# A transformer layer on one core: gating before the root, the shift folded into the router's bias, and a reordered tail

## The chip, the core and the metric

The kernel runs on one core of a Trainium2 chip. The metric is the device time of one execution in microseconds (us); before the change it is 1297.55 us, the median of three runs (1297.47 to 1298.02). The engines are TensorE (PE in the rows; its weight loads are PEld), VectorE (DVE), ScalarE (ACT), GpSimd (POOL) and SyncE (SP), which here only issues DMAs. Each runs its own instructions in program order, and waits on semaphores for the others.

## What is computed

One layer over 128 context tokens and 512 latent tokens of width 1024: token mixing (two kinds of attention, an output projection), then a mixture of experts. What the change touches, cut from the reference:

```python
x = x + g1 * rms_norm(merge_branches(oa, ob, ga, gb, p), p['g_post_mix'])
h = rms_norm(x, p['g_pre_ffn']) * (1 + sc) + sh
lg = (t @ p['w_router_group'] + p['b_router_group'])    # t = h, one row per token
le = (t @ p['w_router_expert'] + p['b_router_expert'])
...
return x + gt * rms_norm(hierarchical_moe(h, p), p['g_post_ffn'])
```

`merge_branches` ends in a product with `w_out`. Each token goes to two of 32 experts, each of them three products with a hidden width of 512; `hierarchical_moe` weighs its two results and adds them. An `rms_norm` needs the mean square of a whole row ahead of its root (a power of -0.5).

## The kernel before

The 640 tokens are NT = 5 tiles of 128 rows, one token on each of 128 partitions. Everything is written out by hand, engine by engine; there is no scheduler, and the order of each engine's work is that of its block of code. The stages that count here:

- **Output projection.** TensorE makes the merged rows in two halves of 512 columns (n = 0 and 1), each by two units of weights and five tiles. Every product is three matmuls (high and low parts of fp32). ScalarE copies a finished tile's half into `yr` and squares it (`merged_rows`, `y_cp`).
- **Between projection and router**, the *row stage* below. For each tile VectorE adds the halves' mean squares; GpSimd takes the root ("merged root", `yrs`); VectorE multiplies by root and gate and adds the old x (`new_x`, two instructions); ScalarE squares the new x (`x1_squares`); VectorE adds EPS; GpSimd takes the second root ("x root", `x1rs`); VectorE scales (`scaled_h`, signals `h2_part`) and adds the shift (`shifted_h`, signals `h2_done`). GpSimd's code has the merged root and the x root of a tile one behind the other, then those of the next tile.
- **Router.** TensorE transposes h (`transpose_h2`, eight matmuls for a tile), ScalarE copies the columns out (`h2_columns`, half of the last tile by VectorE), TensorE multiplies them by the router's weights (`router`), ScalarE copies the 36 logits of each token (`logit_rows`) and TensorE turns them back (`logits`). When all five are there (`rl_done`), VectorE picks the experts and makes the tables of rows to gather.
- **Loads.** SyncE's queue loads 1 MB units of expert weights into six slots. Slots 0 to 2 have their own place. Slots 3 to 5 (`raw_extra`) lie where `yr` and the gate and shift rows are, so their first loads wait until h is stored to memory (`h2_out`) and transposed. GpSimd's gathers read that stored h, and also wait for `h2_out`.
- **Experts.** For each of the 32 experts six weight units are split into high and low parts (ScalarE, then VectorE), and multiplied.
- **Tail.** Five loads of 1 MB bring each token's two results; VectorE weighs the first (`c_part`), adds the weighed second (`c_sum`), ScalarE squares (`c_sq`), GpSimd takes one root over all five tiles (`c_rs`), and VectorE multiplies by root and gate and adds x, in two instructions for each tile; SyncE stores the tile.

## Time and profile before

| | |
|---|---|
| median of three runs | 1297.55 us |
| the profiled execution, its device time | 1295.41 us |
| its span in the trace | 1293.7 us |
| busy: TensorE, VectorE, ScalarE, GpSimd | 1145.2, 848.7, 688.4, 311.1 us |
| mean granted TensorE clock | 0.95 of full speed |

The span runs from the first to the last instruction or transfer of the trace; the profiled execution took 1.7 us more than its span. All positions below are microseconds from the span's start. The row stage and the router lie at about 596 to 638, the experts at about 662 to 1250, the tail at 1255 to the end. A busy share says little here: what counts is, in each stage, which engine the others wait for.

### The profile page before, as it was taken

How to read it: one execution, taken by the hardware profiler on the slowest of the kernel's cores; microseconds unless marked ns; L12 is line 12 of the kernel's file. 1: busy time of each engine (PE TensorE's matmuls, PEld its weight loads, DVE VectorE, ACT ScalarE, POOL GpSimd, SP SyncE). 2: the span in 40 equal slices, each digit the busy share in tenths (PEclk: the TensorE clock that was granted, in tenths of full speed). 3: DMA queues.
4: the chain of work that ended last, by engine and by line, in shares of the span. 5: the costliest groups of instructions: out<-in, count | busy, mean ns of one | idle time of the engine just before them, and what ended most of it. 6: DMA issues, size and time to landing. Idle time of an engine off the chain costs nothing. (4 is left out here: it accounts for less than half of the span.)

```text
span 1293.7 us, 16787 instructions
## 1 busy us (share of the span) xinstructions
PE 1145.2 (89%) x5927; PEld 919.8 (71%) x5927; DVE 848.7 (66%) x901; ACT 688.4 (53%) x781; POOL 311.1 (24%) x306
## 2 busy tenths in 40 slices
PE   4889999999788989998559999999999999999950
PEld 2567788778566777886448788888888888888830
DVE  3543133113787654515739899889898999888936
ACT  3222223223565541234337777877888778877721
POOL 4022021010113002000112443334433344334200
PEclk9889999999898999999769999999999999999985
DMA  9634434555001116421549999999999999999924
GB/s 314 229 98 147 140 119 144 179 171 179 18 1 54 63 33 222 130 73 49 191 171 353 374 376 377 375 364 357 357 364 358 356 356 364 370 352 362 362 67 197
DMA packets 146028, 296.38 MB, mean 229 GB/s; under 512 B 12097, under 2 KB 13250, under 8 KB 145330
## 3 DMA queue, kind: packets, MB, share of 16 engines
q1 hardware_dynamic: 130656, 265.83, 57.7%
q0 software_dynamic: 15152, 29.73, 6.9%
q8 instruction: 36, 0.59, 0.2%
q14 instruction: 22, 0.18, 0.0%
q10 hardware_dynamic: 162, 0.05, 0.0%
HBM read 290.68 MB, written 27.95 MB: 246 GB/s over the span
## 5 line engine op out<-in xcount | busy, mean ns | idle before, releaser
L1192 PE MATMUL psum<-w_hi,act_hi 128*128 128x512 f32 (+1 forms) x1288 | 517.2, 402 | 22.9 <-DVE w_lo L1887 6.3
L1194 PE MATMUL psum<-w_hi,act_lo 128*128 128x512 f32 (+1 forms) x1288 | 502.7, 390 | 0.0
L1193 PE MATMUL psum<-w_lo,act_hi 128*128 128x512 f32 (+1 forms) x1288 | 502.0, 390 | 0.0
L1192 PEld LDWEIGHTS psum<-w_hi,act_hi 128*128 128x128 f32 x1288 | 244.5, 190 | 96.1 <-issue 18.1
L1194 PEld LDWEIGHTS psum<-w_hi,act_lo 128*128 128x128 f32 x1288 | 244.7, 190 | 51.9
L1193 PEld LDWEIGHTS psum<-w_lo,act_hi 128*128 128x128 f32 x1288 | 245.4, 191 | 45.4
L1887 DVE TENSOR_TENSOR w_lo<-raw_extra,w_hi 128x2048 fp32r<-128x2048 f32 x96 | 217.2, 2289 | 45.9 <-ACT w_hi L1082 45.9
L1887 DVE TENSOR_TENSOR w_lo<-raw_mix,w_hi 128x2048 fp32r<-128x2048 f32 x96 | 219.3, 2288 | 12.3 <-ACT w_hi L1082 12.2
L1082 ACT ACTIVATE w_hi<-raw_mix 128x2048 fp32r<-128x2048 f32 x96 | 183.9, 1916 | 27.0 <-PE psum L1194 27.0
L1082 ACT ACTIVATE w_hi<-raw_extra 128x2048 fp32r<-128x2048 f32 x96 | 180.5, 1913 | 7.0 <-PE psum L1194 7.0
L1599 DVE TENSOR_TENSOR w_lo<-raw_mix,w_hi 128x2048 fp32r<-128x2048 f32 (+1 forms) x24 | 52.9, 2202 | 164.5 <-ACT w_hi L882 164.5
L830 POOL DMA_INDIRECT y_scratch<-ysb,scatter_column x32 | 32.6, 1017 | 358.2 <-DVE ysb L2024 347.5
L882 ACT ACTIVATE w_hi<-raw_mix 128x2048 fp32r<-128x2048 f32 (+1 forms) x24 | 44.2, 1842 | 64.1 <-PE psum L1194 37.9
L818 POOL DMA_INDIRECT xg<-h_scratch,gather_column x32 | 69.7, 2177 | 26.1 <-POOL gather_column L815 24.9
L825 POOL COPY scatter_column<-scatter_rows 128x1 uint32 (+1 forms) x32 | 58.1, 1816 | 0.0
L815 POOL COPY gather_column<-gather_rows 128x1 uint32 (+1 forms) x32 | 51.7, 1615 | 21.4 <-DVE gather_rows L1987 16.6
L1013 ACT ACTIVATE rows<-psum,soft 128x640 f32<-128x640 f32 (+3 forms) x80 | 50.7, 641 | 8.1 <-DVE soft L1774 6.1
L1143 ACT ACTIVATE act_hi<-psum 128x512 fp32r<-128x512 f32 x32 | 19.2, 599 | 55.7 <-PE psum L1553 55.7
L1381 PE MATMUL psum<-ident,rows 128*128 128x128 f32 x204 | 38.4, 297 | 10.6 <-DVE pt L1821 4.7
L1772 DVE TENSOR_REDUCE soft<-psum 128x2 f32<-128x1280 f32 (+3 forms) x40 | 44.3, 1109 | 3.7 <-PE psum L1362 1.8
L2004 DVE TENSOR_TENSOR act_lo<-psum,act_hi 128x1024 fp32r<-128x1024 f32 x32 | 39.0, 1219 | 10.9 <-ACT act_hi L1125 10.9
L1125 ACT ACTIVATE act_hi<-psum 128x1024 fp32r<-128x1024 f32 x32 | 32.8, 1025 | 21.2 <-PE psum L1523 21.2
(273 smaller groups left out, 1143.1 us busy)
## 6 DMA issues: line engine op xcount, KB each, us to landing
raw_mix<-in_w_e SPq DMA_DIRECT2D x96, 1024.0 KB, 8.2
raw_extra<-in_w_e SPq DMA_DIRECT2D x96, 1024.0 KB, 8.2
raw_mix<-in_w_in SPq DMA_DIRECT2D x16, 1024.0 KB, 5.8
raw_mix<-in_w_ada SPq DMA_DIRECT2D x16, 1024.0 KB, 7.0
ada_first<-in_w_ada SPq DMA_DIRECT2D x8, 1024.0 KB, 20.3
gates_scratch<-rows POOLq DMA_DIRECT2D x20, 256.0 KB, 3.2
yrow<-gates_scratch POOLq DMA_DIRECT2D x20, 256.0 KB, 4.6
raw_mix<-in_w_out SPq DMA_DIRECT2D x4, 1024.0 KB, 5.1
```

Source lines behind the costliest of these rows:

```text
L815: po.tensor_copy(idx_g[:, par:par + 1], tab_g[:, bass.ds(n, 1)]).then_inc(gi_done, 1)
L818: po.indirect_dma_start(out=xg[:, par * D:(par + 1) * D], out_offset=None, in_=h2_d, in_offset=bass.IndirectOffsetOnAxis(idx_g[:, par:par ...
L825: po.tensor_copy(idx_s[:, par:par + 1], tab_s[:, bass.ds(n, 1)]).then_inc(si_done, 1)
L882: ac.activation(whi(s % HL)[:, :, 0:w], raw(n % RAW_MIX)[:, :, 0:w], ACT.Copy).then_inc(hi_done, 1)
L1013: ac.activation(e[:, m * w:(m + 1) * w], s_view(i)[:, m, :], ACT.Exp, bias=soft[:, 16 * b + m:16 * b + m + 1], scale=SCALE, accum_out=tota ...
L1082: ac.activation(whi(hl), raw(slot), ACT.Copy).then_inc(hi_done, 1)
L1192: pe.matmul(out, a_hi(ka_), w_hi[:, kw, :], start=s, stop=False)
L1193: pe.matmul(out, a_hi(ka_), w_lo[:, kw, :], start=False, stop=False)
L1194: ins = pe.matmul(out, a_lo(ka_), w_hi[:, kw, :], start=False, stop=e)
L1599: ve.tensor_tensor(wlo(s % HL)[:, :, 0:w], raw(n % RAW_MIX)[:, :, 0:w], whi(s % HL)[:, :, 0:w].bitcast(F32), ALU.subtract).then_inc(lo_don ...
L1772: link(ve.reduce_max(so[:, 8:10], s_view(i), AX.X))
L1887: ve.tensor_tensor(wlo(hl), raw(slot), whi(hl).bitcast(F32), ALU.subtract).then_inc(lo_done, 1)
```

## The change

It has three parts.

1. **Row stage.** VectorE now multiplies each half of the merged rows by the gate as soon as it is copied (`gated`, 512 columns), ahead of the root, which makes `new_x` one instruction. The shift is taken off the router's path: TensorE transposes the scaled rows (it waits for `h2_part`), and the shift's part of the logits, shift times the router's weights, is made by eight small matmuls after the first unit of the projection (`rt_mm` then counts one more), copied by ScalarE (`shl`), and added as the bias of `logit_rows`. VectorE still adds the shift to the rows that are stored, but behind each tile's transposes, three of the five behind the copy of the last columns.
2. **Order.** GpSimd takes the merged root of tile i ahead of the x root of tile i - 1. ScalarE splits its second expert unit (`early(0, [1])`) ahead of the second half's rows, and squares and copies in another order. TensorE has the transposes of tile 4 ahead of router 3. VectorE's low part of that second expert unit (`moe_lo(NS + 2, 1, 0)`) moves behind the making of the tables.
3. **Tail.** ScalarE weighs the first result (`first_part`), VectorE adds the second and at once multiplies by the gate into another place (`c_gate`), and behind the root there is one instruction for each tile (`final_rows`).

The diff, without declarations and changed counts:

```diff
-            for i in range(NT):
+            def merged_root(i):
                 po.wait_ge(ysum, i + 1)
                 po.tensor_tensor(stat[:, 8 + i:9 + i], stat[:, i:i + 1], half[:, 0:1], ALU.pow).then_inc(yrs, 1)
+
+            def x1_root(i):
                 po.wait_ge(xsum, i + 1)
                 po.tensor_tensor(stat[:, 40 + i:41 + i], stat[:, 32 + i:33 + i], half[:, 0:1], ALU.pow).then_inc(x1rs, 1)
+
+            merged_root(0)
+            for i in range(1, NT):
+                merged_root(i)
+                x1_root(i - 1)
+            x1_root(NT - 1)
...
@@ -1092,28 +1102,31 @@
                 merged_rows(0, i)
             split_hi(25)
             early(0, [0])
+            ac.wait_ge(rt_mm, 1)
+            link(ac.activation(shl[0:NR, :], bank(7)[0:NR, 0:2], ACT.Copy))
+            early(0, [1])
             for i in range(NT):
                 merged_rows(1, i)
-                if i:
+                if 0 < i < NT - 1:
                     x1_squares(i - 1)
-                if i == 1:
-                    early(0, [1])
 
                     ac.wait_ge(rl_done, i - 1)
-                ac.activation(rlT[:, i % 2 * P:(i % 2 + 1) * P], bank(2 + i % 2)[0:NR, 0:P], ACT.Copy).then_inc(rt_cp, 1)
+                ac.activation(rlT[:, i % 2 * P:(i % 2 + 1) * P], bank(2 + i % 2)[0:NR, 0:P], ACT.Identity, bias=shl[0:NR, min(i, 1):min(i, 1) + 1]).then_inc(rt_cp, 1)
 
             h2_columns(0)
+            x1_squares(NT - 2)
             h2_columns(1)
+            logit_rows(0)
+            h2_columns(2)
             x1_squares(NT - 1)
-            h2_columns(2)
-            logit_rows(0)
+            logit_rows(1)
+            logit_rows(2)
             h2_columns(3)
-            for i in range(1, NT - 1):
-                logit_rows(i)
             h2_columns(NT - 1)
+            logit_rows(3)
             logit_rows(NT - 1)
...
-            for i in range(NT):
+            def first_part(i):
+                ac.wait_ge(x_in[i], 32)
+                y0 = raw_pair(i)[:, 0:D]
+                ac.activation(y0, y0, ACT.Copy, scale=wk[:, i:i + 1]).then_inc(c_part, 1)
+
+            def pair_squares(i):
                 ac.wait_ge(c_sum, i + 1)
                 if i:
                     ac.wait_ge(c_sq, i)
                 ac.activation(pt[:, 1024:2048], raw_pair(i)[:, 0:D], ACT.Square, accum_out=stat[:, i:i + 1]).then_inc(c_sq, 1)
+
+            first_part(0)
+            for i in range(1, NT):
+                first_part(i)
+                pair_squares(i - 1)
+            pair_squares(NT - 1)
...
+                    if n == 0 and u == 0:
+                        shift = modc[:, :].rearrange("p (j s) -> p j s", s=2)
+                        for k in range(KD):
+                            ins = pe.matmul(bank(7)[0:NR, 0:2], wr_v[:, k, :], shift[:, 24 + k, :], start=(k == 0), stop=(k == KD - 1))
+                        ins.then_inc(rt_mm, 1)
 
             def transpose_h2(i):
-                pe.wait_ge(h2_done, i + 1)
+                pe.wait_ge(h2_part, i + 1)
...
             transpose_h2(2)
             router(1)
             logits(0)
-            transpose_h2(3)
             router(2)
             logits(1)
+            transpose_h2(3)
+            logits(2)
+            transpose_h2(4)
             router(3)
-            logits(2)
+            router(4)
             logits(3)
-            transpose_h2(4)
-            router(4)
             logits(4)
...
             moe_lo(NS + 1, 0, 2)
-            ve.wait_ge(y_cp, 5)
+            ve.wait_ge(b_in, 16 * 6)
+
+            def gated(n, i):
+                ve.wait_ge(y_cp, 5 * n + i + 1)
+                half_row = yr[:, i, n * 512:n * 512 + 512]
+                ve.tensor_tensor(half_row, half_row, br_v[:, min(i, 1), n * 512:n * 512 + 512], ALU.mult).then_inc(mix_done, 1)
+
+            for i in range(NT):
+                gated(0, i)
             link(ve.tensor_scalar(stat[:, 48:53], stat[:, 48:53], EPS, None, ALU.add))
+
+            def merged_mean_square(i):
+                ve.wait_ge(y_cp, 5 + i + 1)
+                ve.tensor_tensor(stat[:, i:i + 1], stat[:, 48 + i:49 + i], stat[:, 53 + i:54 + i], ALU.add).then_inc(ysum, 1)
+
+            def mean_square(i):
+                ve.wait_ge(x1sq, i + 1)
+                ve.tensor_scalar(stat[:, 32 + i:33 + i], stat[:, 32 + i:33 + i], EPS, None, ALU.add).then_inc(xsum, 1)
+
+            def new_x(i):
+                ve.wait_ge(yrs, i + 1)
+                ve.wait_ge(x2_in[i], 16)
+                ve.wait_ge(mix_done, 4 * NT + NT + i + 1)
+                ve.scalar_tensor_tensor(xrow[:, i, :], yr[:, i, :], stat[:, 8 + i:9 + i], xrow[:, i, :], ALU.mult, ALU.add).then_inc(x1_done, 1)
 
             def scaled_h(i):
                 ve.wait_ge(x1rs, i + 1)
                 ve.scalar_tensor_tensor(yr[:, i, :], xrow[:, i, :], stat[:, 40 + i:41 + i], br_v[:, 2 + min(i, 1), :], ALU.mult, ALU.mult).then_inc(h2_part, 1)
 
             def shifted_h(i):
-                ve.wait_ge(h2_part, i + 1)
+                ve.wait_ge(h2t_done, 2 * i + 2)
...
-            ve.wait_ge(b_in, 16 * 6)
-            def mean_square(i):
-                ve.wait_ge(x1sq, i + 1)
-                ve.tensor_scalar(stat[:, 32 + i:33 + i], stat[:, 32 + i:33 + i], EPS, None, ALU.add).then_inc(xsum, 1)
-
-            def new_x(i):
-                ve.wait_ge(yrs, i + 1)
-                link(ve.scalar_tensor_tensor(yr[:, i, :], yr[:, i, :], stat[:, 8 + i:9 + i], br_v[:, min(i, 1), :], ALU.mult, ALU.mult))
-                ve.wait_ge(x2_in[i], 16)
-                ve.tensor_tensor(xrow[:, i, :], xrow[:, i, :], yr[:, i, :], ALU.add).then_inc(x1_done, 1)
-
+            merged_mean_square(0)
             for i in range(NT):
-                ve.wait_ge(y_cp, 5 + i + 1)
-                ve.tensor_tensor(stat[:, i:i + 1], stat[:, 48 + i:49 + i], stat[:, 53 + i:54 + i], ALU.add).then_inc(ysum, 1)
-                if i >= 2:
-                    shifted_h(i - 2)
+                gated(1, i)
                 if i:
                     mean_square(i - 1)
                 new_x(i)
+                if i + 1 < NT:
+                    merged_mean_square(i + 1)
                 if i:
                     scaled_h(i - 1)
             mean_square(NT - 1)
-            shifted_h(NT - 2)
+            shifted_h(0)
             scaled_h(NT - 1)
-            shifted_h(NT - 1)
+            shifted_h(1)
             ve.wait_ge(h2t_done, 2 * NT)
-            ve.wait_ge(rt_mm, NT - 2)
+            ve.wait_ge(rt_mm, 1 + NT - 2)
             ve.tensor_copy(h2T_v[(NT - 1) % 2][:, 512:1024], bank(h2_bank(NT - 1, 1))).then_inc(h2t_v, 1)
-            moe_lo(NS + 2, 1, 0)
+            for i in range(2, NT):
+                shifted_h(i)
...
+            moe_lo(NS + 2, 1, 0)
...
-            for i in range(NT):
+            def pair_sum(i):
                 ve.wait_ge(x_in[i], 32)
+                ve.wait_ge(c_part, i + 1)
                 y2 = raw_pair(i)
-                ve.tensor_scalar(y2[:, 0:D], y2[:, 0:D], wk[:, i:i + 1], None, ALU.mult).then_inc(c_part, 1)
-                ve.wait_ge(c_part, i + 1)
                 ve.scalar_tensor_tensor(y2[:, 0:D], y2[:, D:2 * D], wk[:, NT + i:NT + i + 1], y2[:, 0:D], ALU.mult, ALU.add).then_inc(c_sum, 1)
-            ve.wait_ge(c_rs, 1)
+                ve.wait_ge(c_sum, i + 1)
+                ve.tensor_tensor(y2[:, D:2 * D], y2[:, 0:D], g2_v[:, min(i, 1), :], ALU.mult).then_inc(c_gate, 1)
+
+            def final_rows(i):
+                ve.wait_ge(c_rs, 1)
+                ve.wait_ge(c_gate, i + 1)
+                ve.scalar_tensor_tensor(xrow[:, i, :], raw_pair(i)[:, D:2 * D], stat[:, 8 + i:9 + i], xrow[:, i, :], ALU.mult, ALU.add).then_inc(c_out, 1)
+
             ve.wait_ge(g2_in, 32)
             for i in range(NT):
-                y2 = raw_pair(i)
-                ve.scalar_tensor_tensor(y2[:, 0:D], y2[:, 0:D], stat[:, 8 + i:9 + i], g2_v[:, min(i, 1), :], ALU.mult, ALU.mult).then_inc(c_part, 1)
-                ve.wait_ge(c_part, NT + i + 1)
-                ve.tensor_tensor(xrow[:, i, :], xrow[:, i, :], y2[:, 0:D], ALU.add).then_inc(c_out, 1)
+                pair_sum(i)
+            for i in range(NT):
+                final_rows(i)
```

VectorE's instructions of two tiles in the middle of the row stage, before; `yrow` is `yr`, `rows` is x, `brow` holds the gate, scale and shift rows, `stat` the mean squares and roots:

```order
L1904 TENSOR_SCALAR stat<-stat 128x1
L1908 SCALAR_TENSOR_TENSOR yrow<-yrow,stat,brow 128x1024
L1910 TENSOR_TENSOR rows<-rows,yrow 128x1024
L1895 SCALAR_TENSOR_TENSOR yrow<-rows,stat,brow 128x1024
L1914 TENSOR_TENSOR stat<-stat 128x1
L1899 TENSOR_TENSOR yrow<-yrow,brow 128x1024
L1904 TENSOR_SCALAR stat<-stat 128x1
L1908 SCALAR_TENSOR_TENSOR yrow<-yrow,stat,brow 128x1024
L1910 TENSOR_TENSOR rows<-rows,yrow 128x1024
L1895 SCALAR_TENSOR_TENSOR yrow<-rows,stat,brow 128x1024
L1914 TENSOR_TENSOR stat<-stat 128x1
L1899 TENSOR_TENSOR yrow<-yrow,brow 128x1024
```

And with the change, over the same two tiles:

```order
L1946 SCALAR_TENSOR_TENSOR yrow<-rows,stat,brow 128x1024
L1924 TENSOR_TENSOR yrow<-yrow,brow 128x512
L1936 TENSOR_SCALAR stat<-stat 128x1
L1942 SCALAR_TENSOR_TENSOR rows<-yrow,stat,rows 128x1024
L1932 TENSOR_TENSOR stat<-stat 128x1
L1946 SCALAR_TENSOR_TENSOR yrow<-rows,stat,brow 128x1024
L1924 TENSOR_TENSOR yrow<-yrow,brow 128x512
L1936 TENSOR_SCALAR stat<-stat 128x1
L1942 SCALAR_TENSOR_TENSOR rows<-yrow,stat,rows 128x1024
L1932 TENSOR_TENSOR stat<-stat 128x1
```

The shift's addition and the second instruction of the new x are gone from the loop; a half-width product with the gate has come in.

TensorE's instructions from the last projection product to the last logits, before (`ident` marks transposes, `wr` the router's products):

```order
L1466 MATMUL psum<-ident,yrow 128x128 x16
L1475 MATMUL psum<-h2T,wr 36x128 x8
L1466 MATMUL psum<-ident,yrow 128x128 x8
L1475 MATMUL psum<-pt,wr 36x128 x8
L1480 MATMUL psum<-ident,orow 128x36
L1466 MATMUL psum<-ident,yrow 128x128 x8
L1475 MATMUL psum<-h2T,wr 36x128 x8
L1480 MATMUL psum<-ident,orow 128x36
L1475 MATMUL psum<-pt,wr 36x128 x8
L1480 MATMUL psum<-ident,orow 128x36 x2
L1466 MATMUL psum<-ident,yrow 128x128 x8
L1475 MATMUL psum<-h2T,wr 36x128 x8
L1480 MATMUL psum<-ident,orow 128x36
```

And with the change:

```order
L1495 MATMUL psum<-ident,yrow 128x128 x16
L1504 MATMUL psum<-h2T,wr 36x128 x8
L1495 MATMUL psum<-ident,yrow 128x128 x8
L1504 MATMUL psum<-pt,wr 36x128 x8
L1509 MATMUL psum<-ident,orow 128x36
L1504 MATMUL psum<-h2T,wr 36x128 x8
L1509 MATMUL psum<-ident,orow 128x36
L1495 MATMUL psum<-ident,yrow 128x128 x8
L1509 MATMUL psum<-ident,orow 128x36
L1495 MATMUL psum<-ident,yrow 128x128 x8
L1504 MATMUL psum<-pt,wr 36x128 x8
L1504 MATMUL psum<-h2T,wr 36x128 x8
L1509 MATMUL psum<-ident,orow 128x36 x2
```

The transposes of tile 3 now stand behind router 2, and those of tile 4 ahead of routers 3 and 4, which follow each other.

VectorE's end of the program, before, from the last two tiles' sums on:

```order
L2052 TENSOR_SCALAR raw_extra<-raw_extra,pair_weights 128x1024
L2054 SCALAR_TENSOR_TENSOR raw_extra<-raw_extra,pair_weights 128x1024
L2059 SCALAR_TENSOR_TENSOR raw_mix<-raw_mix,stat,last_gate_rows 128x1024
L2061 TENSOR_TENSOR rows<-rows,raw_mix 128x1024
L2059 SCALAR_TENSOR_TENSOR raw_mix<-raw_mix,stat,last_gate_rows 128x1024
L2061 TENSOR_TENSOR rows<-rows,raw_mix 128x1024
```

And with the change:

```order
L2094 SCALAR_TENSOR_TENSOR raw_extra<-raw_extra,pair_weights 128x1024
L2096 TENSOR_TENSOR raw_extra<-raw_extra,last_gate_rows 128x1024
L2101 SCALAR_TENSOR_TENSOR rows<-raw_mix,stat,rows 128x1024 x3
L2101 SCALAR_TENSOR_TENSOR rows<-raw_extra,stat,rows 128x1024 x2
```

Two instructions for each tile behind the root have become one, and the gate's product stands ahead of it.

## Rows read from the trace of the kernel before

**Rows 1.** The stretches view: busy us of each engine, clock, DMA share, GB/s.

```profile
595.00:605.00 10.00, 10.00 (x46) 8.29 (x45) 4.16 (x6) 6.34 (x11) 1.63 (x3) 1.00 0.01 2
615.00:625.00 10.00, 6.03 (x30) 4.96 (x31) 7.60 (x10) 3.10 (x7) 2.10 (x4) 0.54 0.26 105
```

**Rows 2.** The timeline of VectorE: start, us, line, operation, idle before and releaser.

```profile
609.96 1.28 DVE L1908 SCALAR_TENSOR_TENSOR yrow<-yrow,stat,brow 128x1024 f32<-128x1024 f32 x1 [1.17 <-POOL stat L802]
611.28 1.22 DVE L1910 TENSOR_TENSOR rows<-rows,yrow 128x1024 f32<-128x1024 f32 x1
612.42 1.28 DVE L1895 SCALAR_TENSOR_TENSOR yrow<-rows,stat,brow 128x1024 f32<-128x1024 f32 x1
...
616.18 1.29 DVE L1908 SCALAR_TENSOR_TENSOR yrow<-yrow,stat,brow 128x1024 f32<-128x1024 f32 x1 [1.17 <-POOL stat L802]
...
626.25 1.22 DVE L1899 TENSOR_TENSOR yrow<-yrow,brow 128x1024 f32<-128x1024 f32 x1
...
637.54 0.34 DVE L1934 TENSOR_TENSOR router_logits<-psum,br 128x180 f32<-128x180 f32 x1 [0.46 <-PE psum L1480]
```

**Rows 3.** The timeline of ScalarE: merged rows, tiles 0 and 1; squares.

```profile
596.33 0.60 ACT L1061 ACTIVATE yrow<-psum 128x512 f32<-128x512 f32 x1 [11.39 <-PE psum L1194]
...
599.05 0.60 ACT L1061 ACTIVATE yrow<-psum 128x512 f32<-128x512 f32 x1 [1.40 <-PE psum L1194]
...
612.53 1.06 ACT L1068 ACTIVATE pt<-rows 128x1024 f32<-128x1024 f32 x1 [3.88 <-DVE rows L1910]
```

**Rows 4.** The timeline of GpSimd: the x roots of tiles 3 and 4.

```profile
621.33 0.54 POOL L804 TENSOR_TENSOR stat<-stat,half 128x1 f32<-128x1 f32 x1 [5.18 <-DVE stat L1904]
...
626.41 1.46 POOL L804 TENSOR_TENSOR stat<-stat,half 128x1 f32<-128x1 f32 x1 [4.03 <-DVE stat L1904]
```

**Rows 5.** The timeline of TensorE: router products, transposes, first expert product.

```profile
620.94 3.51 PE L1475 MATMUL psum<-h2T,wr 128*36 128x128 f32 x16 [3.96 <-ACT h2T L1075]
...
624.38 1.09 PE L1466 MATMUL psum<-ident,yrow 128*128 128x128 f32 x8
625.40 1.94 PE L1475 MATMUL psum<-pt,wr 128*36 128x128 f32 x16
...
662.50 0.79 PE L1192 MATMUL psum<-w_hi,act_hi 128*128 128x512 f32 x1 [2.44 <-DVE act_lo L2004]
```

**Rows 6.** The timeline of TensorE: four products two columns wide, early on.

```profile
195.06 0.95 PE L1228 MATMUL psum<-fold_parts,modulation_row_parts 128*128 128x2 f32 x8
```

**Rows 7.** Groups by line and form: GpSimd copies one column (busy, mean ns).

```profile
L815 POOL COPY gather_column<-gather_rows 128x1 uint32 x30 | 51.3, 1710 | 4.8 <-PE psum L1523 4.7
```

**Rows 8.** The waits between 680 and 1240: us in total, times, longest.

```profile
ACT w_hi L1082 <- PE psum L1194: 27.0, 61, 0.8
```

**Rows 9.** The timeline of SyncE's queue: the first loads behind the stored h.

```profile
634.25 1.49 SPq L596 DMA_DIRECT2D raw_extra<-in_w_e  x3
```

**Rows 10.** The gathered tile `xg`, all its gathers.

```profile
DMA to landing us min/median/max: 4.4/8.1/8.7
```

**Rows 11.** The timeline of VectorE in the tail.

```profile
1273.39 0.75 DVE L2052 TENSOR_SCALAR raw_extra<-raw_extra,pair_weights 128x1024 f32<-128x1024 f32 x1 [0.38 <-DMA raw_extra<-y_scratch]
1274.18 1.28 DVE L2054 SCALAR_TENSOR_TENSOR raw_extra<-raw_extra,pair_weights 128x1024 f32<-128x1024 f32 x1
1278.27 1.28 DVE L2059 SCALAR_TENSOR_TENSOR raw_mix<-raw_mix,stat,last_gate_rows 128x1024 f32<-128x1024 f32 x1 [2.80 <-POOL stat L695]
...
1289.40 1.22 DVE L2061 TENSOR_TENSOR rows<-rows,raw_extra 128x1024 f32<-128x1024 f32 x1
```

**Rows 12.** The timeline of GpSimd in the tail: the root over five tiles.

```profile
1277.03 1.21 POOL L695 TENSOR_TENSOR stat<-stat,half 128x5 f32<-128x5 f32 x1
```

**Rows 13.** One line's view: ScalarE scales rows by a column, durations min, median, max.

```profile
L919 ACT ACTIVATE rows<-rows,stat x3: 1133/1134/1135, 14.8 to 16.9; 128x1024 f32<-128x1024 f32 x3
```

**Rows 14.** One line's view: the output stores of the tail.

```profile
DMA to landing us min/median/max: 2.6/2.6/2.6
```

**Rows 15.** The stretches view, two microseconds of the output stores.

```profile
1284.00:1286.00 2.00, 0.00 (x0) 0.00 (x0) 1.97 (x3) 0.00 (x0) 0.00 (x0) 0.50 0.65 262
```

20 lines of the change are left out of this document (11 added, 9 removed).

## The prediction

> **What bounds the kernel now.** I read the strip of 40 slices first, then each stage by stretches and timelines. Three parts of the program matter.
>
> The experts, 662 to 1250, hold the most time, and the change edits nothing in them. There ScalarE, when it waits to split a weight unit, waits for TensorE to give a buffer back, never for a load [rows 8]: TensorE sets the pace, and the stage's length stays as it is if it begins earlier and the weights are there. So a gain ahead of it reaches the end in full.
>
> The row stage ahead of it is VectorE's. Between 615 and 625 VectorE is busy for 7.60 of 10 us, ScalarE for 3.10, and TensorE works on at half clock, 0.54 on the mean, after it had stood mostly idle; between 595 and 605, under the projection, TensorE was busy throughout at 1.00 [rows 1]. From one tile's new x (609.96) to the next (616.18) it takes 6.22 us, at whose end VectorE still sits idle for 1.17 us until GpSimd's root [rows 2]. GpSimd could have made it long before: its code has the x root of the tile ahead in front, and so waits 5.18 us for a sum [rows 4]. TensorE delivers a tile each 2.72 us (599.05 less 596.33) [rows 3], so the stage could run more than twice as fast. The stage ends when VectorE takes the last logits, at 637.54 [rows 2]; from there to the first expert product, at 662.50 [rows 5], lie the tables and the first gather.
>
> The tail is one chain: last load, sum, squares, root, then ten VectorE instructions one behind the other, from 1278.27 to 1290.62 (1289.40 and 1.22) [rows 11].
>
> **The row stage, worked out.** Of a tile's VectorE work two instructions of 1.22 leave the loop, the add of old x and the shift [rows 2]; a gate product of half that width comes in, some 0.6. What is left, with starts closer by 0.08 than durations, is gate 0.6, two small ones of 0.1, new x 1.2 and scaling 1.2, thus 3.2. To that comes a wait for the x root. The one root that ran beside a long VectorE instruction took 1.46 instead of 0.54 [rows 4]; that instruction began at 626.25 and ended at 627.47 [rows 2], so the root ended 0.40 behind it. Now nearly every root runs so: 3.2 and 0.4 make 3.6 a tile.
>
> I walked all four engines' new orders with these durations (the same walk over the old orders ends at 637.7, where the trace has 637.54). The small products delay all by their own length. Four with 128-column weights take 0.95 [rows 6]; eight with 36-column weights lie between 0.6 (their weights being narrower) and 1.94, which is eight router products with 128 columns of data [rows 5]. I take 1.2, as for the data they are nearest to the first row. New x of tile 0 then begins at 600.1, and that of tile 4 at 600.1 + 2.7 + 3 x 3.6 = 613.7. Behind it: new x 1.3, squares 1.06 and their read-out, together 1.2 [rows 3], sum and hand-overs 0.7, root 1.5, scaling 1.3, to 619.7; then transposes 1.1 and routers 3 and 4 at 1.9 each [rows 5], to 624.6; copy, last logits and hand-overs 0.7: **625.3**. The order that puts two routers behind the last transposes costs one more router there (1.9), but the copy by VectorE hides in the first of them. Against 637.54 that is 12.3 less, and 11.7 to 13.0 for the bounds of the small products alone.
>
> Costed at nothing: the gate products of the first half (3 us under the projection's second half, where VectorE is idle more than half of the time [rows 1]); the second unit's split by ScalarE, moved to before the second half's rows, where it waits for weights' buffers freed in time (else it would delay the first rows by up to 1.9); the five shifts, of which two lie in waits of VectorE and three (3.5 us) beside routers 3 and 4 (3.8 us). Without that cover they would come in full ahead of the tables. ScalarE's bias in the logits may cost 0.1.
>
> What the shift's move makes late: stored h. Loads for slots 3 to 5 stood at 634.25, 3.3 ahead of the last logits [rows 9]; now the last store is issued at 624.8, the logits' time, and lands 3.3 later (2.6 for a store of this size [rows 14] and a queue of stores). So weights start 6.6 us later against the router, and 6 only ahead of before. SyncE's queue has the later units behind them, and slot 1's reload now waits for the low part that moved behind the tables. All six have landed about when TensorE starts, and none but slot 3's is needed within the first 10 us. But the first gather now meets a full stream. All gathers land in 4.4 to 8.7, median 8.1 [rows 10], and the first one already met one unit of weights; I add 0.3, at most 0.6. GpSimd's clearing of `xg` (it waits for `h2_done`) now falls onto the tables' small VectorE instructions: 0 to 1.8, the latter if they wait for all of it; I take 0.3, as each of them is short.
>
> The clock: behind the projection TensorE gets work of 1.1 to 1.9 us with gaps under a microsecond, and I expect 1.00 to hold up to the last logits. At the experts' start it comes back at half clock either way; by which matmul it rises may move by 1 us. Left at nothing. **Row stage: 12.3 - 0.6 = 11.7, bounds 9.5 to 14.**
>
> **The tail.** ScalarE's weighing has the form of a row that takes 1.13 [rows 13], against 0.75 on VectorE [rows 11], and the last sum begins behind it and one gate product: at 1274.6 instead of 1274.18, so the last squares come 0.4 later. The last gate product (1.2) lies beside those squares, ahead of the root of 1.21 [rows 12]. Final rows begin at 1278.7 instead of 1278.27; five instructions at 1.2 end at 1284.8 instead of 1290.62: 5.9 less. Now stores come each 1.2. At 262 GB/s the transfers took 0.65 of the DMA engines [rows 15], which makes 403 GB/s in full and 1.3 for the 0.52 MB of one tile. From the first store at 1280.0: 2.6 and 4 x 1.3 give 1287.8, where VectorE's last rows alone would give 1287.4, and before it was 1293.3. **Tail: 5.5, bounds 4.5 to 5.9.**
>
> **Sum.** 11.7 + 5.5 = 17.2. Against the profiled execution (span 1293.7, time 1295.41) that gives a span of 1276.5. The median of the runs, 1297.55, is 2.1 above that execution; the saving is the same: **1280.4**.
>
> **A rule against the change.** GpSimd's roots stretch when VectorE is busy, 0.54 to 1.46, and during the experts a copy of one column takes 1.71 on the mean [rows 4, 7]; my sum has 1.5 for most roots. The Trainium skill (GPSIMD Engine Reference, Key points) says that GpSimd shares its SBUF interfaces with VectorE and contends with its instructions in a two-port mode or with two SBUF inputs. New x, gate and scaling all have two SBUF inputs, so by that rule every root may be held; the trace agrees in direction, and no row shows how far it goes when VectorE has no gap. With no root held the walk ends 0.5 earlier; with each held to 2.0, a whole 1.28 and its own time, it ends at 629.2, and the time is 1284.3. How it would be beyond that is the second rival.
>
> **Rivals.**
> - *The weights set the start.* If the experts had no slack in loads, the gain of the row stage would be the loads' 6 us, not 11.7, and the time 1297.55 - 6 - 5.5 = 1286. For it: the loads start late. Against: rows 8, and units not needed at once. 0.12.
> - *GpSimd starved: slower.* Ten roots stand in one line, so the stage ends at about 609 + 10 x the mean root, once that passes 2 us. With 3.4 the whole gain, tail included, is gone; with 4 it is 1304. For it: the stretched rows. Against: the mean there, under instructions of 2.3, is 1.71 [rows 7]. 0.03.
> - *The clock falls during the router.* If TensorE works at half clock from 611 on, router products take 3.51 [rows 5]; walked through, logits end at 635.6, and with the tail the time is 1290. For it: it fell in just this place before. Against: the gaps that did it are gone. 0.08.
> - *It does not do what it says:* with GpSimd or ScalarE in the way the stage keeps its 6.2 and the tail's gain is eaten by stores. Within 0.2%: 0.02.
>
> **How the numbers follow.** The forecast has 0.75. Its own range is 17.2 with the bounds: low 1297.55 - 14 - 5.9 = 1277.6, and 1 less for the clock's rise; high 1297.55 - 9.5 - 4.5 = 1283.6. The 8-in-10 range takes in the weights' rival: 1276.6 to 1287. A difference of 0.2%, 2.6 us, is about what can be told from none. Faster 0.95, same 0.02, slower 0.03.
>
> **What would show it.** New x each 3.6 us and last logits near 625 (with the first row's time the same, within 0.5); roots of 1 to 1.6; TensorE's clock at 1.00 between 608 and 625; first expert product near 651; experts' stage as long as before; final rows 1.2 apart and an end 9.5 us behind the tail's root instead of 15.5. I am wrong if a root takes over 2 us, if the clock falls ahead of 625, or if ScalarE waits for loads.

## The result, and the profile after

| | before | after |
|---|---|---|
| first comparison, median of four runs each | 1297.78 us (1297.47 to 1299.06) | 1276.63 us (1274.88 to 1277.12) |
| ratio after / before, 95% interval | | 0.9834 [0.9819, 0.985] |
| profiled execution, its span | 1295.41, 1293.7 us | 1276.24, 1274.5 us |

Faster by 21.2 us in this comparison, where 17.2 was forecast; the spans of the two traces differ by 19.2 us. Two more comparisons, below, gave 20.8 and 17.8.

**Stretches of the changed kernel** (us busy and, in brackets, instructions of PE, PEld, DVE, ACT, POOL; then granted clock, DMA share, GB/s). They answer to [rows 1]:

```profile
605.00:615.00 10.00, 9.00 (x68) 7.62 (x67) 9.44 (x16) 8.69 (x19) 4.83 (x6) 1.00 0.00 0
615.00:625.00 10.00, 8.20 (x68) 7.16 (x66) 8.67 (x14) 4.67 (x8) 2.92 (x2) 1.00 0.58 233
625.00:635.00 10.00, 1.61 (x30) 1.19 (x30) 8.73 (x27) 0.16 (x1) 0.27 (x2) 0.57 0.78 275
```

TensorE and VectorE are both busy up to the last logits and the clock holds at full (2.4 GHz). It falls to half in the next stretch, when TensorE has nothing but small work for the tables.

**VectorE and GpSimd in the row stage**, timelines of the changed kernel (start, us, engine, line), which answer to [rows 2] and [rows 4]:

```profile
604.37 0.68 DVE L1924 TENSOR_TENSOR yrow<-yrow,brow 128x512 f32<-128x512 f32 x1
604.97 0.14 DVE L1936 TENSOR_SCALAR stat<-stat 128x1 f32<-128x1 f32 x1
605.18 1.28 DVE L1942 SCALAR_TENSOR_TENSOR rows<-yrow,stat,rows 128x1024 f32<-128x1024 f32 x1
606.45 1.28 DVE L1946 SCALAR_TENSOR_TENSOR yrow<-rows,stat,brow 128x1024 f32<-128x1024 f32 x1
608.46 1.28 DVE L1942 SCALAR_TENSOR_TENSOR rows<-yrow,stat,rows 128x1024 f32<-128x1024 f32 x1
...
619.81 3.49 DVE L1950 TENSOR_TENSOR yrow<-yrow,brow 128x1024 f32<-128x1024 f32 x3
623.52 0.35 DVE L1974 TENSOR_TENSOR router_logits<-psum,br 128x180 f32<-128x180 f32 x1 [0.22 <-PE psum L1509]
```

```profile
605.19 0.54 POOL L808 TENSOR_TENSOR stat<-stat,half 128x1 f32<-128x1 f32 x1 [1.47 <-DVE stat L1936]
606.61 1.52 POOL L804 TENSOR_TENSOR stat<-stat,half 128x1 f32<-128x1 f32 x1 [0.88 <-DVE stat L1932]
608.47 0.54 POOL L808 TENSOR_TENSOR stat<-stat,half 128x1 f32<-128x1 f32 x1 [0.34 <-DVE stat L1936]
```

The middle tiles take 3.28 us each (605.18 to 608.46), not 3.6: there is no wait ahead of the scaling at 606.45. The merged root (L804) starts while a scaling runs and ends at 608.13, 0.40 behind that scaling's end (606.45 and 1.28), as in [rows 4]. But the x root (L808) starts within 0.01 us of a new x and takes its bare 0.54. One round earlier the forecast wait is there, and that round took 3.75 us (new x at 601.43 and 605.18):

```profile
601.30 0.15 DVE L1936 TENSOR_SCALAR stat<-stat 128x1 f32<-128x1 f32 x1 [0.32 <-ACT pt L1078]
601.43 1.28 DVE L1942 SCALAR_TENSOR_TENSOR rows<-yrow,stat,rows 128x1024 f32<-128x1024 f32 x1
601.53 1.59 POOL L808 TENSOR_TENSOR stat<-stat,half 128x1 f32<-128x1 f32 x1
603.15 1.29 DVE L1946 SCALAR_TENSOR_TENSOR yrow<-rows,stat,brow 128x1024 f32<-128x1024 f32 x1
```

Here the x root starts 0.10 us into the new x and ends at 603.12; only then can the scaling start. The last three shifts lie beside the last router products. The logits come at 623.52, against 637.54 in [rows 2].

**TensorE**, timeline of the changed kernel; the rows from 606 on answer to [rows 5], the first are the small products:

```profile
565.25 0.72 PE L1483 MATMUL psum<-modc,wr 128*36 128x2 f32 x16
...
606.84 2.04 PE L1495 MATMUL psum<-ident,yrow 128*128 128x128 f32 x16
609.88 1.94 PE L1504 MATMUL psum<-h2T,wr 128*36 128x128 f32 x16 [1.00 <-ACT h2T L1085]
611.75 1.09 PE L1495 MATMUL psum<-ident,yrow 128*128 128x128 f32 x8
...
648.82 0.79 PE L1216 MATMUL psum<-w_hi,act_hi 128*128 128x512 f32 x1 [2.44 <-DVE act_lo L2045]
```

The small products take 0.72 us where 1.2 was put in. One wait of 1.00 us ahead of router 0 does not cost the clock. The first expert product comes 25.30 us behind the logits, 24.96 before.

**The experts' waits**, 665 to 1220, and SyncE's timeline ahead of them, which answer to [rows 8] and [rows 9]:

```profile
ACT w_hi L1092 <- PE psum L1218: 26.8, 61, 0.8
```

```profile
615.90 7.74 SPq L626 DMA_DIRECT2D h_scratch<-yrow  x5
626.68 1.49 SPq L598 DMA_DIRECT2D raw_extra<-in_w_e  x3
```

ScalarE still waits for TensorE alone, in 61 places as before, though slots 3 to 5 are loaded 3.2 us behind the logits instead of 3.3 ahead of them: the weights do not set the start.

**The tail**, timeline of the changed kernel, which answers to [rows 11, 12]:

```profile
1262.20 1.23 DVE L2096 TENSOR_TENSOR raw_extra<-raw_extra,last_gate_rows 128x1024 f32<-128x1024 f32 x1
...
1263.72 1.21 POOL L697 TENSOR_TENSOR stat<-stat,half 128x5 f32<-128x5 f32 x1
1264.97 3.68 DVE L2101 SCALAR_TENSOR_TENSOR rows<-raw_mix,stat,rows 128x1024 f32<-128x1024 f32 x3 [1.54 <-POOL stat L697]
...
1267.47 3.92 SPq L653 DMA_DIRECT2D out_y_sample<-rows  x4
1268.56 2.47 DVE L2101 SCALAR_TENSOR_TENSOR rows<-raw_extra,stat,rows 128x1024 f32<-128x1024 f32 x2
```

Final rows come each 1.2 us. From the issue of the first load to the end it is 32.50 us (1242.00 to 1274.5); it was 37.98 (1255.72 to 1293.7): 5.48 less. Part of that stretch is the loads' own time, which differs from trace to trace. Counted from the first instruction that the last load released it is 20.31 us before and 14.88 now; over all traces below with the old tail 20.25 to 20.33, over the eight with this one 14.81 to 14.92.

### The profile page after: what moved, and what is told of

It reads as the page before. It is cut to its first block and busy times, and to the rows that moved or that the text cites. A ratio compares the mean times of both kernels' runs of the same rounds, so it can differ in the third digit from the quotient of the medians.

```text
span 1274.5 us, 16835 instructions
## 1 busy us (share of the span) xinstructions
PE 1141.1 (90%) x5943; PEld 917.4 (72%) x5943; DVE 844.3 (66%) x901; ACT 694.7 (55%) x787; POOL 316.1 (25%) x306
## 5 line engine op out<-in xcount | busy, mean ns | idle before, releaser
L825 POOL COPY gather_column<-gather_rows 128x1 uint32 (+1 forms) x32 | 52.7, 1648 | 13.8 <-DVE gather_rows L2027 9.7
L1156 ACT ACTIVATE act_hi<-psum 128x512 fp32r<-128x512 f32 x32 | 19.2, 599 | 55.5 <-PE psum L1582 55.5
```

What stands on the lines that cost most here:

```text
L825: po.tensor_copy(idx_g[:, par:par + 1], tab_g[:, bass.ds(n, 1)]).then_inc(gi_done, 1)
```

## The experiments

Executions of one kernel spread by several us, while the row stage, where its code is the same, repeats within 0.02 us from trace to trace. So each trace was cut at the same five places of its timelines: GpSimd's first merged root (A), VectorE taking the last logits (B), first expert product (C), issue of the tail's first load (D), end of the span (E). The other stretches repeat less well: over all kernels here B to C lies between 24.80 and 26.36, C to D between 592.66 and 594.47, and D to E with the changed tail between 31.18 and 33.67. All in us; the ratio is to before on the same chip.

| kernel | A at | A to B | B to C | C to D | D to E | median | ratio, 95% |
|---|---|---|---|---|---|---|---|
| before | 598.02 | 39.52 | 24.96 | 593.22 | 37.98 | | |
| after | 597.82 | 25.70 | 25.30 | 593.18 | 32.50 | 1276.63 | 0.9834 [0.9819, 0.985] |
| e1 before again | 597.71 | 39.53 | 25.36 | 592.66 | 37.34 | 1295.05 | 1.0004 [0.9993, 1.0016] |
| e2 tail only | 598.75 | 39.54 | 24.99 | 593.01 | 32.51 | 1291.19 | 0.9967 [0.9954, 0.998] |
| e3 rows only | 599.71 | 25.69 | 25.53 | 593.18 | 37.59 | 1282.89 | 0.9894 [0.9881, 0.9908] |
| e4 old root order | 598.61 | 28.99 | 26.34 | 593.03 | 32.43 | 1280.63 | 0.9881 [0.9866, 0.9895] |
| e5 after again | 597.63 | 25.70 | 26.36 | 592.98 | 31.63 | 1276.21 | 0.9839 [0.9811, 0.9866] |
| e6 gate undone | 598.63 | 29.87 | 25.18 | 593.30 | 32.52 | 1281.06 | 0.9875 [0.9845, 0.9905] |
| e7 shift on path | 599.71 | 30.44 | 24.80 | 594.47 | 31.18 | 1282.91 | 0.9885 [0.9845, 0.9925] |
| e8 roots by parts | 598.55 | 25.70 | 25.24 | 593.81 | 34.50 | 1278.95 | 0.9857 [0.9827, 0.9886] |
| e9 old PE and ACT order | 596.73 | 31.48 | 25.36 | 593.83 | 32.40 | 1285.95 | 0.9923 [0.9906, 0.994] |
| e10 held store | 599.65 | 25.71 | 25.60 | 593.57 | 33.77 | 1278.93 | 0.9854 [0.9836, 0.9873] |
| e11 two parts | 604.19 | 25.71 | 25.58 | 593.50 | 32.12 | 1278.41 | 0.9854 [0.9838, 0.9871] |
| e12 store after loads | 596.84 | 25.71 | 25.67 | 593.45 | 31.03 | 1275.22 | 0.9856 [0.9833, 0.9879] |
| e13 after again | 601.04 | 25.71 | 25.15 | 593.73 | 33.67 | 1276.91 | 0.9859 [0.9839, 0.9879] |

**e1: the kernel before, unchanged.**

> The kernel before, unchanged, to see how one program's executions differ. The forecast's 1297.55 - 17.2 took over the 2.1 us between the profiled execution and the median of before; with the change the two differ by 0.4 only. Theory A (chance between executions, of any kernel): single times spread over 1295 to 1298, and another profile lands anywhere in it. Rival B (TensorE's clock in the row stage of before, which falls and rises in it): times differ by where the clock rises, and the profile shows half clock for another length than 13.7 us in 600 to 640. Ratio to before 1.000 in both.

1295.05 us in the median of 12 executions, 1293.89 to 1300.92. That spread is wider than expected; its A to B is that of the first trace (39.53 and 39.52) and the clock between 600 and 640 falls and rises as there, which speaks for theory A. The kernel's two sets on this chip have medians 2.2 and 2.7 us below that of the first comparison.

**e2: the tail alone.** All of part 3 of the change, the row stage as before.

> The kernel before with the new tail alone (ScalarE weighs, gate ahead of the root, one instruction behind it). Mine: from the first load's issue to the end 32.5 us instead of 38.0, so 5.5 less, 1292.2, last rows at 1.2 a tile and stores as the bound. Rival: the tail is worth the 2 us more that were measured than traced, 7.5 less, 1290.2.

4.4 us faster than before by the medians (5.5 expected), and D to E 32.51, as in the whole change (37.98 before). The rival's 7.5 us lies outside the interval of the ratio (2.6 to 6.0 us).

**e3: the row stage alone.** Parts 1 and 2, the tail as before.

> The changed kernel with the old tail. Mine: the row stage and what follows it give all the rest, last logits near 623.5 and about 1282.1 (1276.6 + 5.5). If the missing 2 us belong to the tail instead: 1284.

12.7 us faster by the medians; A to B 25.69, that of the whole change (25.70). With e2's 4.4 that makes 17.1 of medians that each are uncertain by 1.5 or so; by stages, 13.8 and 5.5.

**e4: the roots in the old order.**

```diff
-            merged_root(0)
-            for i in range(1, NT):
-                merged_root(i)
-                x1_root(i - 1)
-            x1_root(NT - 1)
+            for i in range(NT):
+                merged_root(i)
+                x1_root(i)
```

> The changed kernel with GpSimd's roots in the old order (x root of a tile ahead of the next tile's merged root). Mine: each new x then waits for two roots in a row; by the walk a tile takes 4.6 instead of 3.3, last logits come 3.8 later (627.5) and the time is 1280.4. Rival: GpSimd is not in the way, since VectorE's own work of 3.2 a tile sets the pace, and TensorE's router work afterwards takes up what is late: within 0.5 of 1276.6.

A to B 28.99, 3.29 more (3.8 expected), at 4.39 a tile: 3.3 us of the stage hang on the order of the roots, and the rival falls. GpSimd's timeline shows it, the x root in front and the merged root right behind it:

```profile
606.73 0.55 POOL L808 TENSOR_TENSOR stat<-stat,half 128x1 f32<-128x1 f32 x1 [3.33 <-DVE stat L1934]
607.25 0.54 POOL L804 TENSOR_TENSOR stat<-stat,half 128x1 f32<-128x1 f32 x1
```

**e5 and e13: the changed kernel, unchanged.**

> The changed kernel once more, unchanged, on the same chip as the three that follow. Theory A (the traces of the two profiled executions hold the whole effect, 19.2 us, and the other 2 us of the first comparison were the executions of before, which spread from 1293.9 to 1300.9 and stood high in that session): the ratio to before is about 0.985, the gain 19 to 19.5 us, and from the first merged root to the last logits the trace shows 25.7 us again, as against 39.5 in before. Theory B (the change gains the 21 us of the first comparison, and the profiled execution of before was a lucky one): ratio 0.9835, a gain over 20.5.

> The changed kernel beside the version above on one chip, in five rounds. Theory A: a gain of 19 to 19.5 us over before as the median of many executions, ratio 0.985, the trace's root to logits 25.7 again. Theory B: ratio 0.9835, gain over 20.5. The share of the 21.2 us that neither trace explains (2.0) is then the spread of the executions ahead of the row stage (the first merged root came between 596.7 and 604.2 us in the eleven kernels run so far, in code that none of them changes but for the small products) or something of the change.

20.8 and 17.8 us faster than before in their own sets, 21.2 in the first. The interval of e5 holds the ratios of both theories, that of e13 (0.9839 to 0.9879) leaves out theory B's 0.9835. The medians of before went from 1294.66 to 1297.78 between sets (four of them on different chips), those of the changed kernel only from 1276.21 to 1276.91; chips and chance are not told apart. All executions together, 58 of before (one stray of 4543.68 us left out) and 13 of the changed kernel, have medians of 1295.69 and 1276.44: 19.25 us, near what the traces say (19.2), though 29 of the 58 ran on a chip where the changed kernel did not. About 19 us is the best figure. Part of the spread is seen ahead of the row stage. Two traces, e1 (A at 597.71) and e11 (A at 604.19), by stretches:

```profile
300.00:400.00 100.00, 83.17 (x569) 67.52 (x567) 71.78 (x175) 54.08 (x124) 15.96 (x32) 0.95 0.10 35
400.00:500.00 100.00, 86.65 (x667) 72.23 (x668) 60.33 (x152) 44.11 (x131) 12.24 (x23) 0.91 0.26 90
```

```profile
300.00:400.00 100.00, 86.94 (x575) 70.73 (x571) 71.37 (x172) 53.85 (x123) 14.74 (x30) 0.90 0.10 38
400.00:500.00 100.00, 84.89 (x644) 70.95 (x643) 60.66 (x153) 45.55 (x135) 12.44 (x23) 0.86 0.21 73
```

The clock granted between 300 and 500, where TensorE works with gaps, is 0.95 and 0.91 in the one, 0.90 and 0.86 in the other, in code that no kernel here changes. It is not all: e3 and e10 have 0.95 and 0.91 there too, and their row stages began 2.0 us behind that of e1.

**e6: the gate behind the root again.**

```diff
-            for i in range(NT):
-                gated(0, i)
...
-                ve.wait_ge(x2_in[i], 16)
-                ve.wait_ge(mix_done, 4 * NT + NT + i + 1)
-                ve.scalar_tensor_tensor(xrow[:, i, :], yr[:, i, :], stat[:, 8 + i:9 + i], xrow[:, i, :], ALU.mult, ALU.add).then_inc(x1_done, 1)
+                link(ve.scalar_tensor_tensor(yr[:, i, :], yr[:, i, :], stat[:, 8 + i:9 + i], br_v[:, min(i, 1), :], ALU.mult, ALU.mult))
+                ve.wait_ge(x2_in[i], 16)
+                ve.tensor_tensor(xrow[:, i, :], xrow[:, i, :], yr[:, i, :], ALU.add).then_inc(x1_done, 1)
...
-                gated(1, i)
```

> The changed kernel with the gate put back into VectorE's row loop as two full rows of work (root times gate, then the sum with x), and no gating by halves; all else as changed. Theory A (VectorE's list of work sets the period of a tile): one 1.2 us instruction more on a row and one 0.7 us instruction less, and the sum can't start before both: period 4.3 instead of 3.28, first merged root to last logits 29.4 us instead of 25.7, so 3.7 us slower than changed. Theory C (GpSimd's two roots set the period, VectorE fits in beside): period stays near 3.3 and the stage within 0.5 us.

A to B 29.87, 4.17 more (3.7 expected), at 4.24 a tile. VectorE's list sets the period; theory C falls. The clock fell here too, behind waits of 2.47 and 1.00 us:

```profile
611.16 1.09 PE L1495 MATMUL psum<-ident,yrow 128*128 128x128 f32 x8 [2.47 <-DVE yrow L1939]
613.25 3.28 PE L1504 MATMUL psum<-h2T,wr 128*36 128x128 f32 x16 [1.00 <-ACT h2T L1085]
616.46 1.37 PE L1495 MATMUL psum<-ident,yrow 128*128 128x128 f32 x8
```

TensorE had no wait from there to the last transposes, at 623.05, for which the scaled rows had been ready since 622.58. So it lost 1.6 us here (3.28 and 1.37 instead of 1.94 and 1.09) and most of that was made good by what it would have waited for anyway; some 0.4, about what the forecast lacks, is left (an estimate from these rows).

**e7: the shift ahead of the transposes again**, without small products and bias.

```diff
                 gated(1, i)
+                if i >= 2:
+                    shifted_h(i - 2)
...
-                pe.wait_ge(h2_part, i + 1)
+                pe.wait_ge(h2_done, i + 1)
```

> The changed kernel with the shift added to every row before its transposes again, and without the sixteen small products and the bias on the logits' copies; all else as changed. Theory A: VectorE's list gets 1.15 us longer a tile, period 4.4 instead of 3.28, first merged root to last logits 28.8 us instead of 25.7, so 3.1 us slower than changed; the small products taken away give back at most the 0.7 us that they last. Theory C (TensorE, which is nearly without gaps from the first router product, sets the end whatever VectorE does): within 1 us of changed.

A to B 30.44, 4.74 more instead of 3.1, at 4.70 to 4.74 a tile instead of 4.4. Its timelines of GpSimd and VectorE:

```profile
612.93 1.54 POOL L808 TENSOR_TENSOR stat<-stat,half 128x1 f32<-128x1 f32 x1 [2.69 <-DVE stat L1929]
```

```profile
612.70 0.15 DVE L1929 TENSOR_SCALAR stat<-stat 128x1 f32<-128x1 f32 x1
612.76 1.28 DVE L1935 SCALAR_TENSOR_TENSOR rows<-yrow,stat,rows 128x1024 f32<-128x1024 f32 x1
613.96 0.17 DVE L1925 TENSOR_TENSOR stat<-stat 128x1 f32<-128x1 f32 x1
614.50 1.28 DVE L1939 SCALAR_TENSOR_TENSOR yrow<-rows,stat,brow 128x1024 f32<-128x1024 f32 x1 [0.38 <-POOL stat L808]
```

Here new x starts 0.06 behind the small instruction (612.76), the x root 0.17 behind new x, and is held to 614.47, so that VectorE waits 0.38: the very wait that the prediction had put into the changed kernel. There, in the middle tiles, new x starts 0.21 behind the small instruction, as it waits for its own gate product just ahead; the root gets in at the same moment and is not held. In the changed kernel's first round the gate product had ended 0.3 us before the small instruction, new x started 0.13 behind that, and the root was held. TensorE waited 3.08 us, came back at half clock, and did tile 1's transposes in 1.97 us instead of 1.1:

```profile
612.84 1.97 PE L1488 MATMUL psum<-ident,yrow 128*128 128x128 f32 x8 [3.08 <-DVE yrow L1943]
614.74 2.42 PE L1497 MATMUL psum<-h2T,wr 128*36 128x128 f32 x16
...
624.80 1.09 PE L1488 MATMUL psum<-ident,yrow 128*128 128x128 f32 x8 [0.82 <-DVE yrow L1943]
```

That did not lengthen the stage: ahead of the last transposes TensorE waits 0.82 us for VectorE again. VectorE's longer round, its waits for the root included, and the last tile's shift are what the stage was longer by.

**e9: TensorE's and ScalarE's lists in the old order**, VectorE, GpSimd and the rest as changed.

```diff
             logits(0)
+            transpose_h2(3)
             router(2)
             logits(1)
-            transpose_h2(3)
-            logits(2)
-            transpose_h2(4)
             router(3)
-            router(4)
+            logits(2)
             logits(3)
+            transpose_h2(4)
+            router(4)
             logits(4)
```

> The changed kernel with TensorE's and ScalarE's lists in the row stage in the order of before (transposes of tile 3 ahead of router 2, those of tile 4 behind router 3 and logits 3; ScalarE's squares of new rows 3 inside the row loop, of rows 4 between the column copies); VectorE, GpSimd, gates by halves and small products as changed. Theory A (with VectorE's list short, TensorE's order sets when the last logits can come): first merged root to last logits 31.0 us as against 25.7, the new x of tile 2 some 1.3 us later because its tile's roots wait for ScalarE; 5.3 us slower than changed. Theory F (the orders only follow VectorE's, and each engine would wait as long in either): within 0.7 us of changed.

The diff shows TensorE's part; ScalarE's squares of tiles 3 and 4 go back to where they were. A to B 31.48, the largest share of all (5.78, expected 5.3). New x keeps its pace of 3.29, also that of tile 2, which had been expected 1.3 later; what is late is behind it. TensorE's timeline, and the stretches around it:

```profile
610.87 2.80 PE L1502 MATMUL psum<-h2T,wr 128*36 128x128 f32 x16 [3.08 <-ACT h2T L1085]
613.60 1.85 PE L1493 MATMUL psum<-ident,yrow 128*128 128x128 f32 x8
```

```profile
605.00:610.00 5.00, 2.79 (x20) 2.19 (x19) 4.93 (x9) 3.62 (x8) 3.24 (x3) 1.00 0.00 0
610.00:615.00 5.00, 4.13 (x23) 3.58 (x24) 4.48 (x7) 3.19 (x7) 2.32 (x3) 0.68 0.00 0
```

A wait of 3.08 us, then half clock for 3 to 4 us: the rival "the clock falls during the router" is real, and the row names what keeps it off: ScalarE's column copy of tile 0, which the change has ahead of the squares of tile 3, and before had behind them. Counted from A, router 0 starts 2.1 us later than in the changed kernel and router 1 3.7 later, after two pieces at half clock; the other 2.1 of the 5.8 come after that. So the larger part goes back to one place in ScalarE's list. What TensorE's order is worth by itself no run shows, as e9 moves both lists.

**e8: roots in three parts in the tail**, ScalarE's squares of pair 0 ahead of the weighing of pair 1, VectorE's final rows of pair 0 ahead of the sum of pair 1.

```diff
-            po.wait_ge(c_sq, NT)
-            rsqrt(stat[:, 8:8 + NT], stat[:, 0:NT], NT, 1.0 / D).then_inc(c_rs, 1)
+            for a, b in ((0, 1), (1, NT - 1), (NT - 1, NT)):
+                po.wait_ge(c_sq, b)
+                rsqrt(stat[:, 8 + a:8 + b], stat[:, a:b], b - a, 1.0 / D).then_inc(c_rs, 1)
```

> The changed kernel with another order in the tail: GpSimd takes the root of pair 0 as soon as its squares are summed, those of pairs 1 to 3 together, that of pair 4 last; ScalarE squares pair 0 before it weighs pair 1; VectorE writes the final rows of pair 0 before it sums pair 1, when it waits for that pair's load anyway. Theory A (VectorE sets the tail's end: 2.5 us for each pair from the second one's landing, then 1.2 for each final row not yet written): one final row moves into the wait for the load and one into the wait for the last root; the last row ends 26.5 us after the first load's issue instead of 29.0, the kernel 2.3 to 3.2 us faster than changed. Theory D (a root is held while VectorE works, so that the one for pairs 1 to 3 ends only 0.4 us after the last gate product, and the last root 0.5 later still): gain 1.5 to 2 us only. Theory E (the stores set the end): no gain.

The last row ended 27.80 us behind D (29.03 in the changed kernel's first trace), but the end came later, not earlier: 34.50; the median is 2.7 us above that of e5, which ran on the same chip. SyncE's waits in its tail (L88 stands for the program's closing code):

```profile
SPq L88 <- PEq L88: 3.5, 1, 3.5
SPq L88 <- DMA out_y_sample<-rows: 2.5, 1, 2.5
```

Behind the last landing the program waited 3.5 us more, 0.2 in every kernel with one root. A to B is the changed kernel's.

**e10: the same with the first store held back.**

```diff
-                sp.wait_ge(c_out, i + 1)
+                sp.wait_ge(c_out, max(i + 1, 2))
```

> The roots by parts once more, with the store of the first final rows held until the second are written, so that no store is among the pairs' loads. Theory A (that store's 512 KB at the loads' pace delayed pairs 3 and 4 by about 1.2 us and so all of VectorE's list behind): last row ends about 27.1 us after the first load's issue, as against 27.8 with the early store and 28.2 to 29.0 as changed. Of the 3.3 us between the last landing and the end, which the roots by parts had more than the changed kernel: gone with the early store (theory G), or still there, as it belongs to the longer program (theory H). By G the kernel is 1 to 2 us faster than changed, by H 1 to 2 slower.

Last row 27.11 behind D, as expected (that store had delayed the loads: ScalarE waited 1.1 us for the fourth pair in e8, 0.3 here), but the closing wait stayed, at 2.2 us: G falls.

**e11: roots in two parts, (0) and (1 to 4).**

> As the held store, with roots in two parts only: pair 0 as soon as it is squared, pairs 1 to 4 together at the end. Theory A: the last root starts as VectorE ends its last gate product and is not held (1.2 us), four final rows come behind it instead of five: last row ends 27.8 us after the first load's issue, 1.2 less than changed, and the kernel is 1.2 us faster, if the end after the last landing is as in the changed kernel (H says it is 3.3 longer whenever the tail's order is another; G says it isn't).

Closing wait 0.2, last row 27.48 behind D, yet D to E 32.12: with five stores issued from 1272.90 on, the end came 8.2 us behind the first of them (1281.1), as in the changed kernel (1266.28 to 1274.5). H falls in its simple form too; the stores set the end.

**e12: two parts, and the first store when the last load has landed.**

```diff
+                if i == 0:
+                    sp.wait_ge(x_in[NT - 1], 32)
                 sp.wait_ge(c_out, i + 1)
```

> Roots in two parts, and the store of the first final rows issued as soon as the last pair's load has landed, where the transfers stood still for 10 us in the changed kernel. Theory I (once VectorE writes a final row each 1.2 us, five stores of 512 KB follow one another without a gap and set the end: it came 8.2 us after the first of the five issues in the changed kernel and in the two-part one alike): four stores are left behind the last root, so the end comes at 30.9 us from the first load's issue, as against 32.5 as changed. Theory K (the program can't end earlier than 8.5 us after GpSimd's last instruction: both three-part kernels ended 8.6 to 8.7 us after it, and SyncE waited there for something of TensorE's queue for 3.5 and 2.2 us after the last landing): GpSimd's last root ends 22.6 us from the load's issue, so the end comes at 31.2 to 31.3 and SyncE's last wait is 0.4 to 0.7 instead of 0.2. Kernel 1.2 to 1.6 us faster than changed. If last rows set the end instead: no more than two parts gave.

Timelines of GpSimd and SyncE, and SyncE's waits:

```profile
1263.05 1.03 POOL L699 TENSOR_TENSOR stat<-stat,half 128x4 f32<-128x4 f32 x1
```

```profile
1258.94 0.34 SPq L655 DMA_DIRECT2D out_y_prompt<-rows  x1
...
1265.42 2.72 SPq L655 DMA_DIRECT2D out_y_sample<-rows  x3
```

```profile
SPq L88 <- PEq L88: 0.6, 1, 0.6
```

D to E 31.03, the shortest of all. GpSimd's last root ended at 1264.08, the span at 1272.7, 8.6 us later; it was 8.7 in both three-part kernels (1269.11 to 1277.8, 1269.65 to 1278.3), and the closing wait is 0.6, as theory K had it. From the end of VectorE's last row it is 3.7, 6.7 and 6.7, so it does not hang on that. Four stores behind one another would have ended about 0.4 earlier. The median is 1.7 us below that of the changed kernel on the same chip (1275.22 and 1276.91), but the intervals to before overlap (0.9833 to 0.9879, 0.9839 to 0.9879), and D to E of the changed kernel itself ranges from 31.63 to 33.67 in three traces: by the times the version is not shown to be faster. The cut behind the loads says more. From the first instruction that the last load released to the end it is 13.75 us, where the eight traces of the changed tail have 14.81 to 14.92, so this one trace is 1.1 us shorter in the part that the edit changes; e11 has 14.66, e8 and e10 16.13 and 16.10.

## Where the prediction held, and which step of it failed

**Right, as it was told.** The mechanism: new x set free from two long instructions and from the x root's place in GpSimd's list; the clock at 1.00 up to the logits; no wait for weights; GpSimd's clearing of `xg` beside the tables without delaying them; experts as long as before (C to D 593.22 and 593.18); the tail 5.48 less, 5.5 forecast.

The 19.2 us of the two traces, by the five cuts: A 0.20 earlier, A to B 13.82, B to C -0.34, C to D 0.04, D to E 5.48. The forecast had 17.2: 11.7 up to the first expert product, where the traces have 13.68, and 5.5 in the tail.

**What failed: the row stage's sum**, in these terms. It put the last logits 12.3 us earlier; they came 14.0 earlier.
- "To that comes a wait for the x root ... 3.2 and 0.4 make 3.6 a tile." This took a wait that one root showed for that of nearly every root. The three rounds took 3.75, 3.28 and 3.29: the wait came in the first alone. In these traces a root was held where VectorE's long instruction had begun 0.10 or more before it, and in the last two rounds both begin at once; e7, where the root begins 0.17 behind, has the wait in every round, with 0.37 to 0.44 behind the first. From new x of tile 0 to that of tile 4 it was 12.95 us (598.80 to 611.75) instead of 13.5 (2.7 and 3 x 3.6, which the text adds up to 613.7 where it is 613.6): 0.55.
- "I take 1.2" for the small products: 0.72 recorded, 0.86 by the spacing of the products around them, so 0.3 to 0.5 less, nearer to the lower bound (0.6) than to the 1.2 that was taken.
- In B to C 0.6 was put in for gather and clearing, and 0.34 was lost in this pair of traces; other pairs range more widely (24.80 to 26.36), so this term is not settled.

Together some 1.2. What the walk had for the end of the stage was right within 0.2 (11.6 from the last new x to the logits, 11.77 measured).

**Of the rest, about 1 is luck of the traces, and 2.0 is the base.** The row stage began 0.2 earlier than in before's trace, though the small products stand ahead of it (0.7 to 0.9); over all traces it began anywhere from 596.73 to 604.19. And "the median of the runs is 2.1 above that execution; the saving is the same": the saving is the same, but the 2.1 was no fixed property of the kernel. In the first comparison before stood at 1297.78, in the other sets at 1294.66 to 1297.01, and its median over all is 1295.69. So 1280.4 stands on a base some 2 us above the kernel's usual time, and of the first comparison's 21.2 us some 2 are that set's; whether its chip or chance made them stays open.

**The rivals.** *Weights set the start*: no, no wait for a load. *GpSimd starved*: no; roots in the row stage took 0.54 to 1.59, none over 2. The rule that the prediction cited (GPSIMD Engine Reference, Key points, in the Trainium skill) speaks of contention, and traces agree in so far as roots that start 0.10 us or more into a two-input instruction are held; they are held to its end and 0.4, and no longer. Roots that start with it are not held. *The clock falls during the router*: not in the changed kernel, but in e6, e7 and e9 it did, behind waits of 2.47 and 1.00 us in the first and of 3.08 in the others. *It does not do what it says*: no.

**What each part carries.** Undone alone, the roots' order costs 3.3 us, the gate 4.2, the shift 4.7, the order of TensorE and ScalarE 5.8: 18.0 in all, where the whole stage gained 13.8. So these prices hold for each part with the others there, and can't be added; no run put one part alone into the kernel before. A likely reason is that the wait of any one engine in the ring (VectorE, GpSimd, ScalarE, TensorE) stops the next tile. The prediction gave the order of TensorE and ScalarE a sentence about one router product; by e9 the two lists together are the largest single share.

**Open.** What TensorE's queue does in the closing code for 8.6 us behind GpSimd's last root was not looked into; three kernels agree on the number, no experiment varied it by itself. That new x's wait for its own gate product is what lets the x root in was read from the gaps (0.21, against 0.13 and 0.06 where the root was held) and not tried alone.
